# A hybrid decoder step on one core: earlier weight splits in the up projection, a later transpose among the gate products, and the last norm's root taken on 128x5 values

## What is computed

```python
g_a, g_b = split(sigmoid(gates))                 # gates: 2 x 1024 columns of the input projection
h = x + (g_a * y_a + g_b * y_b) @ w_o            # y_a: attention branch, y_b: RWKV branch
u = rmsnorm(h, ln2_g) @ w_up                     # 1024 -> 2 * 2816
cv = conv_b + sum(uc[:, i:i + T] * conv_w[i] for i in range(3))
val, gt = split(cv)
out = h + (silu(gt) * val) @ w_down              # 2816 -> 1024
y = out * rsqrt(mean(out * out) + 1e-6) * lnf_g  # final norm, over the 1024 channels of each row
```

## Time and profile before

| what | value |
|---|---|
| median of 3 runs | 1301.92 us |
| the profiled execution's own time | 1303.04 us |
| its span, first to last instruction | 1301.3 us |
| TensorE matmul busy | 1207.9 us (93%), 14362 instructions |
| VectorE, ScalarE, GpSimd busy | 47%, 32%, 33% |
| mean granted TensorE clock | 0.980 |
| the weight and cache loads' DMA queue, share of 16 engines | 45.8% |

### The profile page before, as it was taken

The page is one execution under the profiler, slowest core; times in us unless marked ns, Lnnn a source line. Parts: engine busy times, 40 slices in busy tenths (PEclk is TensorE's granted clock), DMA queues, the critical chain, the costliest instruction groups (busy, mean ns, idle before and its releaser), DMA issues. The chain is left out here.

```text
span 1301.3 us, 33258 instructions
## 1 busy us (share of the span) xinstructions
PE 1207.9 (93%) x14362; PEld 1099.4 (84%) x14362; DVE 618.0 (47%) x1071; ACT 413.9 (32%) x773; POOL 434.4 (33%) x299
## 2 busy tenths in 40 slices
PE   6999998988899899887889999989999999999994
PEld 6998997766666667655689999989999999999994
DVE  6457896444555555674562222244444444440003
ACT  5142331333333333323522222333333333342110
POOL 3333453011101111010143333635555555564440
PEclk9999998999999999999899999989999999999998
DMA  5222215988798889789622222312222222222211
GB/s 212 98 102 66 80 53 227 388 332 326 274 378 318 296 329 376 269 291 378 227 81 82 82 82 82 114 44 82 82 82 82 82 82 83 96 88 88 90 58 73
DMA packets 57251, 216.28 MB, mean 166 GB/s; under 512 B 6609, under 2 KB 6994, under 8 KB 56338
## 3 DMA queue, kind: packets, MB, share of 16 engines
q1 hardware_dynamic: 57106, 214.17, 45.8%
HBM read 207.78 MB, written 6.37 MB: 165 GB/s over the span
## 5 line engine op out<-in xcount | busy, mean ns | idle before, releaser
L667 PE MATMUL ps<-buffer_at 128*128 128x288 f32 (+2 forms) x5760 | 778.4, 297 | 6.5 <-POOL buffer_at L1549 6.5
L667 PEld LDWEIGHTS ps<-buffer_at 128*128 128x128 f32 x5760 | 772.7, 190 | 13.0 <-POOL buffer_at L1549 7.2
L1549 POOL TENSOR_TENSOR buffer_at<-buffer_at 128x1024 fp32r<-128x1024 f32 (+1 forms) x118 | 331.8, 2814 | 340.1 <-ACT buffer_at L1254 339.5
L1254 ACT ACTIVATE buffer_at<-buffer_at 128x1024 fp32r<-128x1024 f32 (+1 forms) x118 | 129.2, 1097 | 287.6 <-PE ps L667 134.5
L1601 POOL TENSOR_TENSOR buffer_at<-buffer_at 128x256 f32<-128x256 f32 x45 | 40.4, 928 | 324.6 <-DVE buffer_at L1844 324.6
L1520 ACT ACTIVATE buffer_at<-buffer_at 128x592 f32<-128x592 f32 x44 | 38.9, 884 | 161.8 <-DVE buffer_at L2233 158.6
L2231 DVE TENSOR_TENSOR buffer_at<-ps,buffer_at 128x512 f32<-128x512 f32 x44 | 30.4, 692 | 125.6 <-PE ps L667 125.5
L1052 PE MATMUL ps<-buffer_at 128*32 128x128 f32 x2048 | 73.7, 283 | 15.5 <-ACT buffer_at L1375 8.7
L1944 DVE TENSOR_REDUCE buffer_at<-ps 128x1 f32<-128x256 f32 (+1 forms) x68 | 28.0, 412 | 103.2 <-PE ps L1019 103.1
L1019 PE MATMUL ps<-buffer_at 128*32 128x256 f32 x1024 | 72.6, 399 | 4.2 <-DMA buffer_at<-in_kvcache 2.9
L1052 PEld LDWEIGHTS ps<-buffer_at 128*32 128x32 f32 x2048 | 54.4, 112 | 25.0 <-issue 11.5
(11 more groups left out here) (247 smaller groups left out, 1280.1 us busy)
## 6 DMA issues: line engine op xcount, KB each, us to landing
buffer_at<-in_kvcache SPq DMA_DIRECT2D x256, 512.0 KB, 6.0
buffer_at<-in_w_up SPq DMA_DIRECT2D x44, 512.0 KB, 3.5
buffer_at<-in_w_in SPq DMA_DIRECT2D x42, 512.0 KB, 3.5
buffer_at<-in_w_down SPq DMA_DIRECT2D x16, 704.0 KB, 4.1
buffer_at<-in_w_br SPq DMA_DIRECT2D x8, 512.0 KB, 3.5
buffer_at<-in_w_o SPq DMA_DIRECT2D x8, 512.0 KB, 3.5
buffer_at<-in_xin SPq DMA_DIRECT2D x4, 576.0 KB, 7.0
buffer_at<-in_xin SPq DMA_DIRECT2D x1, 2304.0 KB, 10.5
```

Of the source, the lines that this page charges most:

```text
L667: ins = e.matmul(out, lhs, rhs[:, cols], start=(start and i == 0), stop=(stop and i == 2))
L1254: e.activation(hi[:, :, :], raw, ACT.Copy).then_inc(w_hi, 1)
L1549: e.tensor_tensor(lo[:, :, :], raw, hi[:, :, :], ALU.subtract).then_inc(w_lo, 1)
```

## The change

Three edits. First, in the up projection, ScalarE's and GpSimd's split of the weights of tile q + 2 now stands ahead of the wait for `up_ev`; ScalarE's waits for `up_mm` of tile q instead, since it overwrites the high part that tile q read. Second, the last transpose is issued after 5 of the 8 k-slices (30 of 48 matmuls) of `gate_part(1, 1)`. Third, in the last norm the sums of squares are made with the squares as the stationary operand and 8 columns of ones as the moving one, so that the batch rows lie on the partitions (five groups of 128, the last one overlapping); the mean, root and reciprocal are taken on 128x5 values; five diagonal matrices are built from them, and a product with ones spreads them over all partitions into PSUM, from where the eight last operations read.

```diff
+        dg = view(31456, 5, P)
...
+            def last_sums():
+
+                e.wait_ge(sq_sum, 18)
+                e.wait_ge(sq_ready, 3 * KT)
+                for t4 in range(5):
+                    t0 = t4 * P if t4 < 4 else T - P
+                    for src, first in ((sqa[2], True), (sqs[2][1], False)):
+                        i = e.matmul(ps[:, 6, 8 * t4:8 * t4 + 8], src[:, t0:t0 + P], ones[:, 0:8], start=first, stop=not first)
+                i.then_inc(sq_used, 1)
+
+            def last_spread():
+
+                e.wait_ge(rs_ready, 2)
+                for t4 in range(5):
+                    out = ps[:, 6, t4 * P:(t4 + 1) * P] if t4 < 4 else ps[:, 7, 0:T - SEQ]
+                    i = e.matmul(out, ones, dg[:, t4, (0, 64)[t4 // 4]:P], start=True, stop=True)
+                i.then_inc(rs_turned, 1)
...
                     gate_part(c + 1, 0, 0, KT)
                     if c == 0:
+                        gate_part(1, 1, 0, 5)
                         out_turn(PAIRS - 1)
-                    gate_part(c + 1, 1, 0, KT)
+                        gate_part(1, 1, 5, KT)
+                    else:
+                        gate_part(c + 1, 1, 0, KT)
...
-            square_sums(2)
+            last_sums()
+            last_spread()
...
+                n = q + 2
+                if n < 2 * NF:
+                    e.wait_ge(up_mm, q + 1)
+                    w_split(wuh[n % 2], wr[n % 4], w_u[n % 4], 16 * (n // 4 + 1))
                 e.wait_ge(up_ev, q + 1)
                 e.wait_ge(up_st, q + 1)
                 if q >= 4:
                     e.wait_ge(up_h, j - 1)
                 e.activation(cc[s], cu[s][:, 2:594], ACT.Identity, bias=pcol("cb", col), scale=pcol("cw2", col)).then_inc(up_c0, 1)
-                n = q + 2
-                if n < 2 * NF:
-                    w_split(wuh[n % 2], wr[n % 4], w_u[n % 4], 16 * (n // 4 + 1))
-                else:
+                if n >= 2 * NF:
...
+                n = q + 2
+                if n < 2 * NF:
+                    w_split(W_UP + n, wl[n % 4], wr[n % 4], wuh[n % 2])
                 e.wait_ge(up_ev, q + 1)
...
+            def last_rstd():
+
+                own_ = Line(e, own["norm"], 4)
+                e.wait_ge(sq_used, 3)
+                own_.did(e.tensor_scalar(rsc[:, 0:5], ps[:, 6, 0:40].rearrange("p (a b) -> p a b", a=5)[:, :, 0], 1.0 / D, EPS, ALU.mult, ALU.add))
+                own_.settle()
+                e.sem_inc(ms_ready, 1)
+                e.wait_ge(rt_ready, 3)
+                own_.did(e.reciprocal(rsc[:, 0:5], rsc[:, 0:5]))
+                own_.settle()
+                for t4 in range(5):
+                    i = e.tensor_scalar(dg[:, t4, :], ident, rsc[:, t4:t4 + 1], None, ALU.mult)
+                i.then_inc(rs_ready, 1)
...
-            rstd(2)
-            normed("lnf")
+            last_rstd()
+            e.wait_ge(rs_turned, 2)
+            for k in range(KT):
+                e.scalar_tensor_tensor(out=xn[:, k, :], in0=x[:, k, :], scalar=pcol("lnf", k),
+                                       in1=ps[:, 6:8, :].rearrange("p b n -> p (b n)")[:, 0:T],
+                                       op0=ALU.mult, op1=ALU.mult).then_inc(xn_ready, 1)
```

More of the change, by code:

```diff
@@ L1248, in root @@
                 e.wait_ge(ms_ready, n + 1)
-                e.activation(rs, rs, ACT.Sqrt).then_inc(rt_ready, 1)
+                r = rs if n < 2 else rsc[:, 0:5]
+                e.activation(r, r, ACT.Sqrt).then_inc(rt_ready, 1)
             def w_split(hi, raw, arrived, n):
@@ L1662, in rstd @@
                 own_.settle()
[L1664 to L1672, removed]
             la = Line(e, own["attn"])
```

## The result

| | before | changed |
|---|---|---|
| median, 8 runs each on one chip | 1303.32 us | 1294.83 us |
| lowest and highest | 1301.61 to 1307.07 | 1291.74 to 1303.11 |
| ratio, 95% interval | | 0.9942 [0.9918, 0.9966] |
| profiled execution, own time and span | 1303.04, 1301.3 | 1297.48, 1295.7 |

The kernel is faster by 7.6 us by the ratio (interval 4.4 to 10.7). I had forecast 10.0 and a time of 1291.9 in a range up to 1294.5; 1294.83 lies outside, and so the prediction was wrong, though not in its direction.

The account below looks back on a forecast made before the run. TensorE, busy 93% of the span, was taken as the bound, with gains only at its stalls and the tail. 7.4 + 0.2 + 2.4 = 10.0 us gave a median of 1291.9, range 1290.6 to 1294.5.

Parts of the forecast that it names:

- Edit 1: Start of the up projection: tile 2's wait (5.11 us) and the half clock behind it (2.29) go, 7.40 us gained.
- the reciprocal passed GpSimd by: Up projection start: GpSimd's split assumed undelayed beside VectorE's 3.75 us reciprocal; rival of a delay, 15%, 1293.7 or 1296.0.
- Steady part: Later up-projection tiles: cost 0, since TensorE's 6.40 us per tile hides VectorE's taps standing still behind GpSimd's split.
- The slower rival: Up projection: splits choke VectorE's taps in a closing loop, 6.75 us per tile, kernel at 1307; chance 4%.
- Edit 2: Last transpose: gain only 0.2 us, as gate (1, 1) waits for its own low weights from GpSimd until 665.11.
- since the idle time is: Last transpose: the clock behind the stall stays the same because the idle time does; about 1.6 us of half clock.
- Edit 3: Tail, last norm: 1.94 us from a shorter chain and 0.44 from the eight last operations, together 2.4 us.
- I take full clock: Tail: the five spreading matmuls run at full clock in 1.3 us; half clock would take 1.1 more.
- the other terms of the chain: Tail: sums, mean, root, reciprocal, diagonals and hand-overs; with the spreading they add to 5.63 us, against 7.57 before.
- the 0.44 us for reading PSUM: Tail: the eight last operations take 756 ns each as L1799, instead of 811, by reading PSUM; 0.44 us less.
- The sum: Whole kernel: 7.4 + 0.2 + 2.4 = 10.0 us gained, median 1291.9.
- half clock at the spreading: Tail rival: two TensorE pauses close together bring half clock at the spreading, 1293.0; chance 18%.

Follow-up runs that it names:

- a run of its own: Changed kernel with 96 instead of 8 columns of ones in the last sums; one profiled execution, no ratio; first sum to first last operation 5.70 us.
- the pause filled: Changed kernel with 8 matmuls of 128 columns that serve nothing, issued between the last sums and the spreading; ratio 0.9947 [0.9925, 0.9969].

## Why the prediction was wrong

- **Edit 1**, forecast 7.40: measured 7.0. The stall and the clock loss behind it both went, and the reciprocal passed GpSimd by; the term was 0.4 too large. I took tile 1 to last 6.40 from its first matmul, and a tile's output to start 6.44 behind it. But the first matmul behind the sums of squares is followed 0.33 us later by the next, and not 0.12, so that in the changed kernel tile 2 starts 6.61 behind tile 1; and the output of tile 2 starts 6.60 behind its first matmul. Together that is the 0.4. The profile's own 4.73 us of idle time was the right size of the stall. The clock's return moves this term too: without the edit the 26.64 us are 26.71 in the run with the transpose alone and 27.16 in the one with the tail alone.
- **Steady part**, forecast 0: right, with GpSimd's start at 1.14 us (forecast 1.1) and the taps' end at 5.4 (forecast 5.6). The slower rival's loop did not close.
- **Edit 2**, forecast 0.2: right; the wait went from 4.34 to 4.18. The loss of 0.9 in the profile is from how long the clock stays low, which scatters with and without the edit. I had taken it as equal, "since the idle time is"; the runs show that equal idle time does not give an equal stretch.
- **Edit 3**, forecast 2.4: measured 0.9. This is the step that failed, in two terms. "I take full clock" for the spreading was wrong by 1.1 us. I looked at the length of the pause alone and at a stall of 1.65 that had done no harm, and did not see that the new sums put 2.4 us of work with 8 columns ahead of the pause. At full clock the chain took 5.70 in a run of its own, so the other terms of the chain were right. And the 0.44 us for reading PSUM did not come in either order of the operands (806 to 809 ns each, not 756): the price from L1799 did not carry over. The trace of the kernel before already held the reason. Groups by line and form:

```profile
L1770 DVE SCALAR_TENSOR_TENSOR buffer_at<-buffer_at 128x576 f32<-128x576 f32 x4 | 3.3, 819 | 0.1
L1750 DVE SCALAR_TENSOR_TENSOR buffer_at<-buffer_at,ps 128x576 f32<-128x576 f32 x4 | 3.2, 804 | 0.0
...
L1777 DVE SCALAR_TENSOR_TENSOR buffer_at<-buffer_at 128x576 f32<-128x576 f32 x4 | 3.0, 748 | 0.0
```

  L1799 and L1777 take their scalar as a constant in the program (`-SCALE`, `-1.0`) and need 756 ns with PSUM and 748 without; L1750 and L1770 take a column of the parameter table (`pcol`), one value for each partition, and need 804 with PSUM and 819 without. The eight last operations use `pcol`, before (811) and after (806). So the 50 ns that I put down to PSUM go with the kind of scalar; no run changes that alone.
- **The sum** at its measured sizes is 7.0 + 0.2 + 0.9 = 8.1 us, inside the interval of 4.4 to 10.7. The rival "half clock at the spreading" was the true case, at 18%, and missed the 0.8 us of the other terms. Its reason, "two pauses of TensorE close to each other", was not the cause: with the pause filled the clock was down as well. The chances did not add up either: the list has 4% for the slower case, the paragraph behind it 4% for slower and 3% for no change. The base was 1.4 us higher in the runs of the result (1303.32) than the three I had, and runs of one kernel spread by several us, from the stage ahead of all edits; a range whose upper end was 2.6 us above the forecast did not allow for that. With the measured 8.1 and the base of 1303.32 the sum gives 1295.2, against 1294.83 measured.

## What to carry to other kernels

When a wait is to be covered, list everything that the covering work itself waits for: its weights, its bank, and the engine order that each of these stands in; here all three ended within a few microseconds, and each edit uncovered the next. A split of weights, or any other preparation, should be issued on what it truly needs (the buffer is free) and not behind a chain that only happens to stand ahead of it; here only the first two of 42 paid. And where matmuls on a latency path are shrunk, look at the granted clock of what follows: here 8 columns instead of 96 saved 0.07 us, as the weight loads filled the time either way, and cost 1.1 us behind them. And when the price of an operation is taken from another line, compare all its operands, the scalar too, and look for a second line that differs in one of them only.

## What the runs showed that I had not expected

- Ten pairs of float32 records took 2.37 us with 8 columns and 2.44 with 96, and only with 96 did the clock stay up for the work behind them. With 8 columns it fell even where TensorE did not pause behind them.
- VectorE's busy time can grow by some 75 us (618.0 to 692.7 with the moved splits alone) by standing still behind GpSimd, with an operation of 128x64 at 2.43 us, and the kernel does not notice.
- Behind a stall of 4.2 to 4.5 us the clock came back 3.1 to 6.0 us after TensorE's new start. A stall of 2.9 us lowered it in one execution and not in another, and so did one of 1.75.
- The multiply with a scalar and a second tensor (`scalar_tensor_tensor`) on 128x576 took 748 to 756 ns with a constant and 804 to 819 with one scalar per partition, from SBUF and from PSUM alike.
- In one of the thirteen profiled executions (before, changed, and eleven experiments), the gate and output products ran at 6.24 us per tile instead of 6.40, some 4.7 us in all over 1400 matmuls, with the same program on TensorE; start-to-start times there alternate between 132 and 128 ns, where they otherwise repeat as 131, 131, 131, 140. Why stays open.
